# The query's rotary rotation: VectorE writes 32 rows across instead of a TensorE product

## The reference

```python
q = (rms_norm(q_lat, g_q_lat) @ w_q_up).reshape(B, S, MLA_HEADS, MLA_QK_DIM)
k = jnp.concatenate([k_nope, k_r], axis=-1)
q = rms_norm(q, g_q_mla); k = rms_norm(k, g_k_mla)
q = jnp.concatenate([q[..., :128], apply_rope(q[..., 128:], pos)], axis=-1)
k = jnp.concatenate([k[..., :128], apply_rope(k[..., 128:], pos)], axis=-1)
o = causal_attention_blocks(q, k, v)

def apply_rope(x, pos):      # x1, x2: the first and the second 32 of the 64
    return concatenate([x1 * cos - x2 * sin, x2 * cos + x1 * sin])
```

## Time and profile before

| | us |
|---|---|
| three timed runs | 1596.10, 1598.25, 1600.08 |
| median | 1598.25 |
| profiled execution, first to last instruction (its span) | 1599.0 |
| TensorE busy | 1573.0 |
| VectorE busy | 1154.1 |
| ScalarE busy | 862.4 |
| GpSimd busy | 151.6 |

### The profile page before, as it was taken

The page is one execution under the profiler, slowest core; times in us unless marked ns, Lnnn a source line. Parts: engine busy times, 40 slices in busy tenths (PEclk is TensorE's granted clock), DMA queues, the critical chain, the costliest instruction groups (busy, mean ns, idle before and its releaser), DMA issues.

```text
span 1599.0 us, 24289 instructions
## 1 busy us (share of the span) xinstructions
PE 1573.0 (98%) x9650; PEld 1400.7 (88%) x9650; DVE 1154.1 (72%) x1696; ACT 862.4 (54%) x1321; POOL 151.6 (9%) x164
## 2 busy tenths in 40 slices
PE   8998999989999999999999999999999999999999
PEld 6787889988999999988799888888888888888887
DVE  6797867877778886759778777777777777455544
ACT  6855546767665555655556454544444444444442
POOL 0000000321221220034213000000000000000000
PEclk9999999999999999999999999999999999999999
DMA  9999975533457774343244545555455454555552
GB/s 373 369 343 349 365 285 209 188 114 121 180 189 267 285 272 179 132 158 132 97 144 178 189 170 199 184 186 210 172 197 191 179 211 175 205 199 185 198 196 105
DMA packets 47825, 331.02 MB, mean 207 GB/s; under 512 B 5281, under 2 KB 6689, under 8 KB 8417
## 3 DMA queue, kind: packets, MB, share of 16 engines
q1 hardware_dynamic: 45184, 312.20, 53.5%
q0 software_dynamic: 2240, 17.04, 2.8%
q10 hardware_dynamic: 290, 0.25, 0.1%
HBM read 327.37 MB, written 2.10 MB: 206 GB/s over the span
## 4 chain that ended last, share of the span: by engine, by line
PE 89%; DVE 5%; DMA 3%; ACT 2%; issue 1%; POOL 0%; SPq 0%; ACTq 0%; DVEq 0%; POOLq 0%
PE ps L1173 20%; PE ps L1174 11%; PE ps L1169 9%; PE ps L1170 8%; PE ps L1171 8%; PE ps L1228 5%; PE ps L1227 5%; PE ps L1226 5%; PE ps L1216 4%; PE ps L1217 3%; PE ps L1218 3%; DVE wl L1916 2%; DMA raw<-in_wts 1%; DMA xs<-in_xN 1%; PE ps L1384 1%; PE ps L1351 1%
## 5 line engine op out<-in xcount | busy, mean ns | idle before, releaser
L1916 DVE TENSOR_TENSOR wl<-raw,wh 128x1024 fp32r<-128x1024 f32 x512 | 626.2, 1236 | 282.4 <-ACT wh L1519 281.9
L1519 ACT ACTIVATE wh<-raw 128x1024 fp32r<-128x1024 f32 x512 | 531.3, 1054 | 377.2 <-PE ps L1228 130.6
L1173 PE MATMUL ps<-hA,wh 128*128 128x512 f32 x1408 | 488.7, 390 | 0.0
L1174 PE MATMUL ps<-hA,wl 128*128 128x256 f32 x1408 | 397.0, 282 | 0.0
L1173 PEld LDWEIGHTS ps<-hA,wh 128*128 128x128 f32 x1408 | 264.2, 188 | 55.3
L1174 PEld LDWEIGHTS ps<-hA,wl 128*128 128x128 f32 x1408 | 266.1, 189 | 0.0
L1169 PE MATMUL ps<-hA,wh 128*128 128x256 f32 x752 | 219.5, 292 | 0.0
L1170 PE MATMUL ps<-hA,wh 128*128 128x256 f32 x752 | 211.7, 282 | 0.0
L1171 PE MATMUL ps<-hA,wl 128*128 128x256 f32 x752 | 211.7, 282 | 0.0
L1169 PE MATMUL ps<-hB,wh 128*128 128x256 f32 x576 | 164.4, 285 | 0.8 <-DVE work L2362 0.4
L1170 PE MATMUL ps<-hB,wh 128*128 128x256 f32 x576 | 161.1, 280 | 0.0
(11 more groups left out here) (303 smaller groups left out, 2077.9 us busy)
## 6 DMA issues: line engine op xcount, KB each, us to landing
raw<-in_wts SPq DMA_DIRECT2D x256, 1024.0 KB, 4.8
raw<-in_ada SPq DMA_DIRECT2D x36, 1024.0 KB, 6.1
side<-in_ada POOLq DMA_DIRECT2D x12, 1024.0 KB, 8.5
work<-in_memN SPq DMA_DIRECT2D x2, 1024.0 KB, 8.9
xs<-in_xN POOLq DMA_DIRECT2D x1, 2048.0 KB, 20.6
xs<-in_xT POOLq DMA_DIRECT2D x2, 1024.0 KB, 7.8
out_rows<-xs SPq DMA_DIRECT2D x8, 256.0 KB, 2.4
wp<-in_dt SPq DMA_DIRECT2D x8, 128.0 KB, 2.7
```

Of the source, the lines that this page charges most:

```text
L1173: e.matmul(ps[bank][:, :], w1, hl, start=first, stop=False)
L1174: i = e.matmul(ps[bank][:, T:2 * T], w2, hl[:, 0:T], start=False, stop=last)
L1519: e.activation(wh[:, h % WS, :], raw[:, n % RAW, part * HALF:(part + 1) * HALF], ACT.Copy).then_inc(s_hi)
L1916: e.tensor_tensor(wl[:, h % WS, :], src, wh[:, h % WS, :].bitcast(F32), ALU.subtract).then_inc(s_lo)
```

## The change

The stage `rot` and its product are gone. VectorE takes its place in stage `u`: it multiplies the first 32 rotary rows by the sine and writes the result to the second 32 rows of the target, and multiplies the second 32 rows by minus one and by the sine and writes to the first 32. Both read SBUF, where the old one read PSUM, and both follow "gr". GpSimd's cosine product now waits for VectorE's second instruction, since it overwrites in place what VectorE reads. The planner's tables lose the stage, VectorE's cost of `u` becomes 0.9 for 0.45, and the hold of head 3's `rot` goes to its `sq`.

```diff
-MLA = ("sq", "rot", "u", "ss", "r1", "rstd", "norm") + SOFTMAX + ("hi", "lo")
+MLA = ("sq", "u", "ss", "r1", "rstd", "norm") + SOFTMAX + ("hi", "lo")
-    mla=dict(sq="a2.0", rot="p.5", u="d.45 o2", ss="p1.8", ...
+    mla=dict(sq="a2.0", u="d.9 o2", ss="p1.8", ...
-    ... ('mla', 3): {'rot': 1.16},
+    ... ('mla', 3): {'sq': 1.16},
@@ tensor, mla
-                if k == "rot":
-                    e.wait_ge(*after(t, "act", "gr"))
-                    e.matmul(ps[bank][:, 0:T], cs[half, CST["rot"][0]:CST["rot"][1]], qrh, start=True, stop=True).then_inc(mark(t, "pe", "rot"))
@@ vector, mla
+                base = 64 * (h % 2)
+                one, two = slice(base, base + 32), slice(base + 32, base + 64)
                 if k == "u":
-                    e.wait_ge(*after(t, "pe", "rot"))
-                    e.tensor_tensor(B["r"][half, T:512], pb[half, 0:T], cs[half, CST["sin"][0]:CST["sin"][1]], ALU.mult).then_inc(mark(t, "dve", "u"))
+                    e.wait_ge(*after(t, "act", "gr"))
+                    e.tensor_tensor(B["r"][two, T:512], qrs[h // 4][one, j % 2, :], cs[one, sin0:sin1], ALU.mult).then_inc(mark(t, "dve", "u1"))
+                    e.scalar_tensor_tensor(out=B["r"][one, T:512], in0=qrs[h // 4][two, j % 2, :], scalar=-1.0, in1=cs[two, sin0:sin1], op0=ALU.mult, op1=ALU.mult).then_inc(mark(t, "dve", "u"))
@@ gpsimd, mla
                 if k == "u":
-                    e.wait_ge(*after(t, "pe", "rot"))
+                    e.wait_ge(*after(t, "dve", "u"))
                     e.tensor_tensor(qrh, qrh, cs[half, CST["cos"][0]:CST["cos"][1]], ALU.mult).then_inc(mark(t, "pool", "cos"))
                     e.wait_ge(*after(t, "pool", "cos"))
-                    e.wait_ge(*after(t, "dve", "u"))
```

More of the change, by code:

```diff
@@ L97 @@
     rk={0: "d.45 a.4", 1: "p.43 d1.3"},
-    mla=dict(sq="a2.0", rot="p.5", u="d.45 o2", ss="p1.8", **HEAD_RSTD, **(CAUSAL | dict(scores="p1.7"))),
+    mla=dict(sq="a2.0", u="d.9 o2", ss="p1.8", **HEAD_RSTD, **(CAUSAL | dict(scores="p1.7"))),
     mem=dict(sq="a.4", ss="p.43", r1="d.45", rstd="a.85", norm="d1.9", **(CAUSAL | dict(scores="p.85", max="d1.2", exp="a1.6", scale="a1.2", pt="a.63", pv="p.85"))),
@@ L205 @@
     ('mem', 3): {'add': -4.01, 'ss': 0.64}, ('mla', 1): {'sq': -1.72, 'pt': -0.76, 'exp': -1.8},
-    ('mla', 2): {'max': -1.51, 'lo': -1.2, 'norm': 4.28}, ('mla', 3): {'rot': 1.16},
+    ('mla', 2): {'max': -1.51, 'lo': -1.2, 'norm': 4.28}, ('mla', 3): {'sq': 1.16},
     ('mla', 4): {'max': -2.22, 'r1': 3.17, 'rstd': 2.42, 'pt': 2.23, 'pv': -0.84}, ('mla', 5): {'u': 2.23, 'rstd': 0.55},
@@ L2230, in mla @@
                 s = h % 4
-                B, pb = lset[s], ps[4 + s]
-                half = slice(64 * (h % 2), 64 * (h % 2) + 64)
+                B, pb, j = lset[s], ps[4 + s], h // 2
+                base = 64 * (h % 2)
+                one, two = slice(base, base + 32), slice(base + 32, base + 64)
                 q, kh = qns[h // 4][:, s, :], kns[h // 4][:, s, :]
+                sin0, sin1 = CST["sin"]
                 if k == "u":
-                    e.wait_ge(*after(t, "pe", "rot"))
-                    e.tensor_tensor(B["r"][half, T:512], pb[half, 0:T], cs[half, CST["sin"][0]:CST["sin"][1]], ALU.mult).then_inc(mark(t, "dve", "u"))
+                    e.wait_ge(*after(t, "act", "gr"))
+                    e.tensor_tensor(B["r"][two, T:512], qrs[h // 4][one, j % 2, :], cs[one, sin0:sin1], ALU.mult).then_inc(mark(t, "dve", "u1"))
+                    e.scalar_tensor_tensor(out=B["r"][one, T:512], in0=qrs[h // 4][two, j % 2, :], scalar=-1.0, in1=cs[two, sin0:sin1], op0=ALU.mult, op1=ALU.mult).then_inc(mark(t, "dve", "u"))
                 if k == "r1":
```

## The result

The changed kernel takes 1616.05 us (median of six runs, 1614.88 to 1623.00) against 1599.58 for the kernel before in the same session (six runs, 1596.10 to 1600.93). The ratio is 1.0117 [1.0102, 1.0132]: the change costs 16 us by the medians and 19 by the ratio, where 5.4 were to be gained.

What follows compares the result with a forecast made beforehand. TensorE was taken as the bound, busy 98% of the span. Removing 5.7 us and adding 0.3 gave -5.4 us, from 1598.25 to 1592.8 (-0.34%), with a range of 1590.8 to 1598.

Steps and rivals of the forecast that it cites:

- what bounds the kernel: TensorE bounds the edit's stretch and 900 to 1200 us, with weights supplied ahead, so time saved around 750 reaches the end.
- TensorE, removed: Rotation products of eight heads, standing at seven places, go from TensorE: 7 x 0.82 = 5.7 us saved, between 4.4 and 6.8.
- The list of beats: Planner's order from 690 to 830 us: without eight stages, later ones shift by a few blocks, costing TensorE +0.3 us.
- the leads at two seams: TensorE's wait for line 2362 near 780 us, and head 5's low part 2.3 us ahead near 830; +0.3 us together.
- Rival (a): Late stages issued with no blocks between, or a `norm` ahead of line 2362, cost 1 to 4 us; 1595.5, chance 0.30.
- rival (c): Head 5's whole softmax sent bare near 830 us, ten stages, 10 us; slower at 1600.6, up to 1603, chance 0.08.
- VectorE, added: Stage `u`: two 32-row instructions replace one, +0.5 us a head, 3.9 in all, 0 to 12, none on TensorE's path.
- GpSimd and the new waits: GpSimd's cosine starts up to 0.9 us later for a head, covered by blocks between `u` and `scores`; costed at nothing.
- The hold rule on neighbouring instructions: VectorE instructions starting in another partition quarter wait for earlier ones: 1.9 us more on VectorE, no change to TensorE's sum.

Runs made afterwards that it cites:

- the list's own kernel: The instructions of the kernel before on the changed kernel's list of beats, TensorE's product issued at the beat of `u`; 1620.57 us, ratio 1.0139.
- the two early kernels: Changed arithmetic on the old list, `u` issued earlier on VectorE alone (1598.32 us, ratio 0.9998), or for heads 0 to 3 on GpSimd too (1594.33, 0.9969).
- the first filled one: The changed kernel with 16, 5 and 62 matmuls that nobody reads put into TensorE's longest waits; 1616.45 us, ratio 1.0096 against the kernel before.

## Why the prediction was wrong

- The first part, **what bounds the kernel**, was right: TensorE is the bound, and a difference in this stretch reaches the end unchanged, 300.00 of 300 us busy from 900 on.
- **TensorE, removed**: 5.7 us forecast, 5.3 by the account of the kernel without the product, and the -5.7 also closes the other accounts. Right. 
- **The list of beats** is the step that failed. It took +0.3 us, from the leads at two seams in the trace of before. But that trace shows the leads of the old list, and the new list is another one: of the heads' stages, 116 moved, by 13 blocks on average. The measured price is +21.2 us in the list's own kernel. The prediction had the sentence that later stages "shift by a few blocks", which is far too few, and took the price of a shift from the slack of the present order, which holds only if the order stays. The list could have been written out from the planner's rules, which need no chip; then the bare stages would have been seen.
- The mechanism that came was named: last stages of a head that `until` leaves bare. **Rival (a)** had it with a chance of 0.30, priced at 1 to 4 us, and **rival (c)** with 0.08, at the second seam, priced at 10. It came at the first seam, with heads 0 and 1, where TensorE stood for 1.68, 3.17 and 4.97 us between 785 and 797.5, 9.8 in all. That this is near (c)'s 10 is luck, since (c) was worked out for another head's whole softmax at the other seam. No rival had the waits of 2.2 and 1.9 us that end at 722 and 733.6, or the clock, so even (c)'s upper end, 1603, is 13 us below the measured time.
- **VectorE, added**: +0.5 a head was nearly right without GpSimd (0.41 to 0.42 each, so +0.4), and beside GpSimd the instructions are inside the upper bound: medians of 0.72 and 0.61 for heads 0 to 3, up to 0.89. The claim that none of it lies on TensorE's path was wrong, and this is a second step that failed. On the old list TensorE's waits grew from 0.4 to 5.6 us, of which 1.3 came with the removal alone, and with the clock's 1.7 that ate the product's gain. A wait of 2.2 to 3.6 us that ends between 720 and 726 is in every kernel that has the new arithmetic at the beat `u`, whatever its list (2.25 in the changed one), and in those with the old arithmetic it is 0.9 at most. The argument was the 39.2 us of ScalarE's waits; they show a lead of weights, not one of evacuations, and it was an evacuation (line 2299) that came late.
- **GpSimd and the new waits**, costed at nothing: wrong by 3.6 us, the difference of the two early kernels in the table. With VectorE's part early, `scores` waits for GpSimd for 1.9 us and the clock falls once, which costs 1.8; with GpSimd's part early too, both are gone.
- The hold rule on neighbouring instructions, said not to move TensorE's sum, was borne out in its 0.75 for 0.72; its share in the late evacuation wasn't measured apart.

Not tried: which single moved stage costs most in the new list, and the changed list with the stages of heads 0 and 1 put back.

## What to carry to other kernels

Where a planner writes the order of work, a removed stage or a changed cost is two changes: price the instruction on the old order, and write out the new order and read it at every seam before pricing that; a shift that changes no instruction cost 8 to 10 us here. Removing 0.82 us of TensorE time seven times gave most of its worth (4.5 of 5.7 us in the stretch) only when the work that replaced it was issued where VectorE and GpSimd had idle time. A new wait of TensorE should be priced with the half clock that may follow it: here it added 4 to 11 us to 16.4 us of waits.

## What the hardware showed that was not expected

- Around waits of TensorE of 1 to 5 us the granted clock was half for 3.4, 10.2 or 13.7 us, with blocks 0.21 apart instead of 0.12; the four kernels with 1.7 us of waits or less in all show no half clock in 690 to 900, and neither does the first filled one, with 8.6. Two executions of one program with the same waits differed by 7 us through this alone.
- An instruction of VectorE over 32 rows with both inputs in SBUF takes 0.41 to 0.42 us while GpSimd is idle, as one over 64 or 128 rows does. Beside GpSimd most take 0.72 to 0.90, and some 0.42 to 0.51. The one of before, which read PSUM, took 0.408 to 0.428 for all eight heads, the four of heads 0 to 3, which run beside GpSimd, among them. The change alters the place of the inputs and the number of rows together. That the place matters is suggested by line 2242, 128 rows with its inputs in SBUF, which took 0.48 us and, while GpSimd was working, 0.97; no run separates the two.
